# A decoder step on one Trainium2 core: the feed-forward gate and up products made as 2x2 block products with seven multiplications

## The reference, cut to what matters

```
x <- x + 1/2 * SwiGLU_1(RMSNorm(x))
x <- x + mixer(RMSNorm(x)) @ w_out          (attention branches and a pooling mixer)
x <- x + 1/2 * SwiGLU_2(RMSNorm(x))
y = RMSNorm_final(x)

def swiglu_ffn(x, g, w_gate, w_up, w_down):
    h = rmsnorm(x, g)
    return (jax.nn.silu(h @ w_gate) * (h @ w_up)) @ w_down
```

## Time and profile before

| | |
|---|---|
| median of 3 runs | 2870.1 us (2867.83 to 2872.59) |
| span of the profiled execution | 2868.9 us (no time of its own beside the span is given; it lies 1.2 us under the median) |
| stage `f1` | 456.7 to 1241.5 us |
| stage `f2` | 2078.0 us to the end |
| PE busy / DVE busy / ACT busy | 92% / 52% / 31% of the span |
| mean granted PE clock | 0.975 of full |

### The profile page before, as it was taken

One profiled execution on the slowest core, in us unless ns is written; L12 is line 12 of the kernel. 1 busy time (PEld: TensorE's weight loads), 2 busy tenths in 40 slices (PEclk: granted clock), 3 DMA queues, 4 the chain that ended last, 5 costly groups with the idle time before them and its releaser, 6 DMA issues. The chain is left out here.

```text
span 2868.9 us, 44901 instructions
## 1 busy us (share of the span) xinstructions
PE 2649.2 (92%) x17616; PEld 2498.9 (87%) x17616; DVE 1484.9 (52%) x2887; ACT 885.1 (31%) x1570; POOL 384.7 (13%) x427
## 2 busy tenths in 40 slices
PE   4999998999999999999978888777999999999997
PEld 4888887999999999988966666556999999999997
DVE  5444445554444444464147768555464444444445
ACT  4656655111111111032246656444221111111112
POOL 4444441000000000000012222452000000000001
PEclk9999999999999999999979979899999999999999
DMA  4131313211111110021311010586031111111101
GB/s 180 64 125 64 125 56 119 74 46 58 55 47 44 44 44 29 15 100 43 101 62 45 24 44 34 185 279 226 16 88 45 45 55 46 44 44 44 51 15 61
DMA packets 171831, 206.88 MB, mean 72 GB/s; under 512 B 15342, under 2 KB 153455, under 8 KB 169002
## 3 DMA queue, kind: packets, MB, share of 16 engines
q1 hardware_dynamic: 161026, 144.91, 16.3%
q0 software_dynamic: 10672, 60.19, 5.7%
HBM read 191.39 MB, written 18.01 MB: 73 GB/s over the span
## 5 line engine op out<-in xcount | busy, mean ns | idle before, releaser
L464 ACT ACTIVATE f_act_gate<-f_act_gate 128x352 f32<-128x352 f32 x132 | 65.8, 498 | 1185.3 <-DVE f_act_gate L572 1185.2
L589 DVE SCALAR_TENSOR_TENSOR trunk<-f_down,trunk 128x352 f32<-128x352 f32 x528 | 275.9, 524 | 205.3 <-PE f_down L114 205.3
L112 PE MATMUL f_down<-f_a_hi,f_wd_hi 128*128 128x352 f32 x1056 | 341.1, 323 | 0.0
L114 PE MATMUL f_down<-f_a_hi,f_wd_lo 128*128 128x352 f32 x1056 | 340.3, 322 | 0.0
L113 PE MATMUL f_down<-f_a_lo,f_wd_hi 128*128 128x352 f32 x1056 | 339.3, 321 | 0.0
L112 PE MATMUL cs_sum<-cs_x_hi,cs_w_hi 128*128 128x256 f32 (+1 forms) x768 | 230.3, 300 | 33.0 <-DVE cs_x_lo L1184 21.6
L114 PE MATMUL cs_sum<-cs_x_hi,cs_w_lo 128*128 128x256 f32 (+1 forms) x768 | 218.0, 284 | 0.0
L113 PE MATMUL cs_sum<-cs_x_lo,cs_w_hi 128*128 128x256 f32 (+1 forms) x768 | 217.6, 283 | 0.0
L1041 POOL TENSOR_TENSOR cs_x_lo<-cs_x,cs_x_hi 128x516 fp32r<-128x516 f32 x128 | 170.9, 1335 | 235.4 <-ACT cs_x_hi L1098 235.4
L114 PEld LDWEIGHTS f_down<-f_a_hi,f_wd_lo 128*128 128x128 f32 x1056 | 199.1, 189 | 0.0
L113 PEld LDWEIGHTS f_down<-f_a_lo,f_wd_hi 128*128 128x128 f32 x1056 | 198.7, 188 | 0.1
(11 more groups left out here) (421 smaller groups left out, 6745.6 us busy)
## 6 DMA issues: line engine op xcount, KB each, us to landing
f_gu_raw<-in_w_ffn_gate_dram SPq DMA_DIRECT2D x44, 512.0 KB, 4.3
f_gu_raw<-in_w_ffn_up_dram SPq DMA_DIRECT2D x44, 512.0 KB, 5.7
as_pages<-in_cache_kv_slc_dram SPq DMA_DIRECT2D x128, 128.0 KB, 4.0
as_pages<-in_cache_kv_slc_dram POOLq DMA_DIRECT2D x128, 128.0 KB, 4.0
at_spread<-saved_rows SPq DMA_DIRECT2D x16, 768.0 KB, 3.9
in_w_raw<-in_w_ffn_down_dram SPq DMA_DIRECT2D x11, 1024.0 KB, 5.0
f_wd_raw<-in_w_ffn_down_dram SPq DMA_DIRECT2D x11, 1024.0 KB, 5.0
x_saved<-trunk SPq DMA_DIRECT2D x2, 2112.0 KB, 14.8
```

Source lines behind the costliest of these rows:

```text
L112: pe.matmul(out, w_hi, x_hi, start=first, stop=False)
L114: return pe.matmul(out, w_lo, x_hi, start=False, stop=last)
L464: act.activation(act_gate[:, b, :], act_gate[:, b, :], ACT.Silu).then_inc(silu_done, 1)
L589: dve.scalar_tensor_tensor(xT[:, m, chunk(c)], down_bank[n % 4][:, 0:CH], 0.5, xT[:, m, chunk(c)], ALU.mult, ALU.add).then_inc(down_free, 1)
```

## The change

For one hidden tile the gate and up weights are four blocks: gate and up (two block rows), model channels 0 to 511 and 512 to 1023 (two block columns, `KH` = 4 k-tiles each). Token thirds 0 and 1 form the other 2x2 block matrix. Their product is made with seven block products on sums of blocks instead of eight; third 2 stays plain. So:

- Weights: eight forms of 4 k-tiles per hidden tile (four raw blocks and four sums or differences made on DVE by `sum_w`), each with its own high part (`high_w`, ACT) and low part (`low_w`, DVE), in a ring of four slots. Before it was 16 k-tiles with one high and one low instruction.
- Tokens: six block operands `b_sum` and a seventh, `last_sum`, made once per stage and kept on chip with their high and low parts (`high_b`, `low_b`), and `s_hi`, `s_lo` for third 2. They replace the `h_hi`, `h_lo` of all thirds, so the out-projection stage no longer makes those of thirds 0 and 1.
- PE: 7 x 12 matmuls for the blocks and 48 for third 2, 132 per tile; 264 + 144 per pair.
- Results: copies of two banks on ACT (`base`, `fifth`), five more additions on DVE per tile. The activation's high part goes from DVE to ACT (`high_a`).
- Order: the loops are written out for all 11 pairs. Between the steps of the activation DVE and ACT make the next tile's first four forms. Down products begin with third 1 (`order_of`), in the last pair with third 0, and each third waits for its `low_a` (`a_ready`).
- `f1_wd_lo` now lies in the memory of `in_w_raw`, so the input projection's first load waits for the last down product.
- The Newton step has one instruction less; the final norm's rows have a tile each.

The core of the diff, engine by engine. SP, the loads of a tile's weights and the next stage's first load:

```diff
+def load_half(v, j, k, split):
+    if v:
+        sp.wait_ge(w_lo_done, 8 * v - 8 + split)
+    sp.dma_start(gu_raw[:, j, k:k + KH], (wg_v, wu_v)[j][:, k:k + KH, v, :]).then_inc(
+        raw_landed[j][k // KH], 16)
+
+def load_raw(v):
+    load_half(v, 0, 0, 4)
+    load_half(v, 0, KH, 6)
+    load_half(v, 1, 0, 7)
+    load_half(v, 1, KH, 8)
...
+    sp.wait_ge(down_done, DOWNS * PAIRS)
+    sp.wait_ge(up_far_done, FT)
     sp.dma_start(next_load[0], next_load[1]).then_inc(next_landed, 16)
```

ACT, for each tile:

```diff
+def high_w(v, i):
+    n = 8 * v + i
+    if i in SUM_OF:
+        act.wait_ge(w_summed, 4 * v + SUM_OF[i][1])
+    else:
+        act.wait_ge(raw_landed[RAW_OF[i][0]][RAW_OF[i][1] // KH], 16 * v + 16)
+    if n >= 4:
+        act.wait_ge(product_done, event((n - 4) // 8, END[(n - 4) % 8]))
+    act.activation(w_hi[:, i % 4], form(i), ACT.Copy).then_inc(w_hi_done, 1)
...
+for g in range(FT):
+    act.wait_ge(product_done, event(g, 1))
+    if g:
+        act.wait_ge(act_done[0], g)
+    act.activation(base, bank_1, ACT.Copy).then_inc(first_copied, 1)
+    high_w(g, 4)
+    act.wait_ge(product_done, event(g, 3))
+    if g:
+        act.wait_ge(act_done[1], g)
+    act.activation(fifth, bank_5, ACT.Copy).then_inc(fifth_copied, 1)
+    high_w(g, 5)
+    high_w(g, 6)
+    if g == 0:
+        norm.root(act, 2)
+    high_w(g, 7)
+    if g % 2 == 0:
+        act.wait_ge(wd_landed, 16 * (g // 2) + 16)
+        act.activation(wd_hi[:], wd_raw, ACT.Copy).then_inc(wd_hi_done, 1)
+    silu(g, 0)
+    silu(g, 2)
+    silu(g, 1)
+    if g + 1 < FT:
+        high_w(g + 1, 0)
+    high_a(g, 1)
+    if g + 1 < FT:
+        high_w(g + 1, 1)
+        high_w(g + 1, 2)
+    high_a(g, 0)
+    if g + 1 < FT:
+        high_w(g + 1, 3)
+    high_a(g, 2)
```

DVE, ahead of the first tile:

```diff
+low_w(0, 0)
+with_first_half(1, 0, 1)
+low_b(0, 1)
+low_s(0)
+sum_w(0, 1)
+low_w(0, 1)
+dve.wait_ge(scaled, 2)
+dve.wait_ge(b_made, 1)
+dve.tensor_tensor(b_sum[:, 3], b_sum[:, 5], b_sum[:, 1], ALU.subtract).then_inc(b_made, 1)
+low_b(1, 2)
+with_first_half(2, 5, 2)
+sum_w(0, 2)
+low_w(0, 2)
+dve.wait_ge(b_made, 3)
+low_b(2, 3)
+if not prepared:
     norm.mean_square(dve, sum_bank, 0)
+sum_w(0, 3)
+low_w(0, 3)
+dve.wait_ge(scaled, 3)
+dve.wait_ge(b_made, 2)
+dve.tensor_tensor(last_sum[:], b_sum[:, 4], b_sum[:, 3], ALU.subtract).then_inc(b_made, 1)
+low_b(3, 4)
+if not prepared:
     norm.invert(dve, 0)
     norm.mean_square(dve, sum_bank, 1)
+dve.wait_ge(b_made, 4)
+low_b(4, 5)
+low_b(5, 6)
+low_b(6, 7)
+low_s(KH)
+if not prepared:
+    norm.invert(dve, 1)
```

DVE, for each tile:

```diff
+for g in (2 * q, 2 * q + 1):
+    more = g + 1 < FT
+    sum_w(g, 5)
+    low_w(g, 4)
+    low_w(g, 5)
+    low_w(g, 6)
+    if g == 0:
+        norm.mean_square(dve, sum_bank, 2)
+    dve.wait_ge(product_done, event(g, 5))
+    dve.wait_ge(first_copied, g + 1)
+    dve.tensor_tensor(base, base, bank_6, ALU.add).then_inc(base_done, 1)
+    dve.wait_ge(base_done, g + 1)
+    dve.tensor_tensor(above, base, bank_7, ALU.add).then_inc(above_done, 1)
+    low_w(g, 7)
+    if g == 0:
+        dve.wait_ge(above_done, 1)
+        norm.tmp = far
         norm.invert(dve, 2)
...
+    dve.wait_ge(above_done, g + 1)
+    dve.wait_ge(fifth_copied, g + 1)
+    dve.tensor_tensor(fifth, above, fifth, ALU.add).then_inc(up_far_done, 1)
+    dve.wait_ge(product_done, event(g, 6))
+    if g:
+        dve.wait_ge(a_ready[0], g)
+    dve.tensor_tensor(near, bank_1, inv[:, chunk(0)], ALU.mult).then_inc(gate_scaled[0], 1)
+    dve.wait_ge(product_done, event(g, 7))
+    if g:
+        dve.wait_ge(a_ready[2], g)
+    dve.tensor_tensor(third, bank_gate, inv[:, chunk(2)], ALU.mult).then_inc(gate_scaled[2], 1)
+    if g % 2 == 0:
+        dve.wait_ge(wd_hi_done, q + 1)
+        dve.tensor_tensor(wd_lo, wd_raw, wd_hi[:].bitcast(F32), ALU.subtract).then_inc(wd_split, 1)
+    rescale(g, 0)
+    rescale(g, 2)
+    dve.wait_ge(product_done, event(g, 8))
+    if g:
+        dve.wait_ge(a_ready[1], g)
+    dve.tensor_tensor(far, base, bank_5, ALU.add).then_inc(far_summed, 1)
+    dve.wait_ge(far_summed, g + 1)
+    dve.tensor_tensor(far, far, inv[:, chunk(1)], ALU.mult).then_inc(gate_scaled[1], 1)
+    if more:
+        sum_w(g + 1, 1)
+        low_w(g + 1, 0)
+    rescale(g, 1)
+    activate(g, 1, fifth, up_far_done, g + 1)
+    if more:
+        low_w(g + 1, 1)
+        sum_w(g + 1, 2)
+    dve.wait_ge(product_done, event(g, 10))
+    dve.wait_ge(far_summed, g + 1)
+    dve.tensor_tensor(base, base, bank_7, ALU.add).then_inc(up_near_done, 1)
+    activate(g, 0, base, up_near_done, g + 1)
+    low_a(g, 1)
+    if more:
+        low_w(g + 1, 2)
+        sum_w(g + 1, 3)
+    activate(g, 2, bank_up, product_done, event(g, 11))
+    low_a(g, 0)
+    if more:
+        low_w(g + 1, 3)
+    low_a(g, 2)
```

PE, for each tile (`strassen` and `plain` are 12 matmuls each, `begin` waits for the form's low part):

```diff
+def tile(g):
+    q, first = g // 2, g % 2 == 0
+    begin(g, 0)
+    if g and first:
+        pe.wait_ge(down_free, DOWNS * q - 1)
+    elif g:
+        pe.wait_ge(gate_scaled[0], g)
+    strassen(g, 0, 0, bank_1, True)
+    if g:
+        pe.wait_ge(gate_scaled[2], g)
+    plain(g, 0, 0, bank_gate, True)
+    if g == 0 and not prepared:
+        norm.total(pe, sum_bank, 1)
+    begin(g, 1)
+    if g:
+        pe.wait_ge(far_summed, g)
+    strassen(g, 1, 1, bank_5, True)
+    begin(g, 2)
+    if g:
+        pe.wait_ge(up_near_done, g)
+    strassen(g, 2, 2, bank_7, True)
+    begin(g, 3)
+    if g and first:
+        pe.wait_ge(down_free, DOWNS * q)
+    elif g:
+        pe.wait_ge(base_done, g)
+    strassen(g, 3, 3, bank_6, True)
+    if g == 0:
+        norm.total(pe, sum_bank, 2)
+    begin(g, 4)
+    pe.wait_ge(first_copied, g + 1)
+    strassen(g, 4, 4, bank_1, False)
+    plain(g, 4, KH, bank_gate, False)
+    begin(g, 5)
+    pe.wait_ge(fifth_copied, g + 1)
+    strassen(g, 5, 5, bank_5, False)
+    begin(g, 6)
+    if g:
+        pe.wait_ge(act_done[2], g)
+    plain(g, 6, 0, bank_up, True)
+    begin(g, 7)
+    pe.wait_ge(above_done, g + 1)
+    strassen(g, 7, 6, bank_7, False)
+    plain(g, 7, KH, bank_up, False)
```

More of the change, by code:

```diff
@@ L346, in stage_ffn @@
[L346 to L363, removed]
+            h_hi, h_lo, next_norm, next_gain, next_w, wd_lo, next_load, next_landed = ahead
@@ new lines, in stage_ffn @@
+        base, fifth, far, near = [mem.sb(scope, f"{name}_{part}", [P, CH])[:] for part in ("base", "fifth", "far", "near")]
+        above = spare_temp if ahead else mem.sb(scope, name + "_above", [P, CH])[:]
+        third = norm.var[:]
+        norm.tmp = above
+        doubles = [mem.ps(scope, f"{name}_bank{i}", (P, 2 * BANK)) for i in range(4)]
+        singles = [x[:, i * BANK:(i + 1) * BANK] for x in doubles for i in range(2)]
+        bank_1, bank_6, bank_5, bank_7, bank_gate, bank_up = [x[:, 0:CH] for x in singles[2:8]]
@@ new lines, in stage_ffn @@
+        down_done, down_free = mem.sem(name + "_down_done"), mem.sem(name + "_down_free")
+        gate_of = (near, far, third)
+        if ahead:
+            next_norm.sq = next_sq[:]
+        if finish:
+            flat_rows = b_sum[:].rearrange("p f k n -> p (f k n)")
+            rows = [flat_rows[:, t * D_MODEL:(t + 1) * D_MODEL] for t in range(TT - 1)]
+            rows.append(gu_raw[:, 0].rearrange("p k n -> p (k n)"))
+            fin.use([doubles[2 + t % 2] for t in range(7)] + doubles[0:2], rows)
@@ new lines, in scale, with high_b @@
+                def scale(i, c, k0):
+                    act.wait_ge(norm.gain_in, 16)
+                    for k in range(KH):
+                        last = act.activation(b_sum[:, i, k], xT[:, k0 + k, chunk(c)], ACT.Copy,
+                                              scale=norm.gain[:, k0 + k:k0 + k + 1])
+                    last.then_inc(scaled, 1)
+                def high_b(i, ready, count):
+                    act.wait_ge(ready, count)
+                    whole, high, _ = operand(i)
+                    act.activation(high, whole, ACT.Copy).then_inc(b_hi_done, 1)
@@ L514, in _ @@
                 if finish:
[L515 to L517 removed]
+                    act.wait_ge(product_done, event(FT, 0))
                     for t in range(6):
@@ new lines, in low_w, with with_first_half @@
+                def low_w(v, i):
+                    dve.wait_ge(w_hi_done, 8 * v + i + 1)
+                    dve.tensor_tensor(w_lo[:, i % 4], form(i), w_hi[:, i % 4].bitcast(F32),
+                                      ALU.subtract).then_inc(w_lo_done, 1)
+                def with_first_half(out, other, ready):
+                    dve.wait_ge(scaled, ready)
+                    for k in range(KH):
+                        made = dve.scalar_tensor_tensor(b_sum[:, out, k], xT[:, k, chunk(1)], norm.gain[:, k:k + 1],
+                                                        b_sum[:, other, k], ALU.mult, ALU.subtract)
+                    made.then_inc(b_made, 1)
@@ new lines, in low_b, with low_s @@
+                def low_b(i, count):
+                    whole, high, low = operand(i)
+                    dve.wait_ge(b_hi_done, count)
+                    dve.wait_ge(b_made, READ_BY[i])
```

(8 more changed lines are left out.)

585 lines of the change are left out of this document (281 added, 304 removed).

## The result

| | before | after |
|---|---|---|
| median | 2868.97 us (2867.60 to 2872.59, 4 runs) | 2895.18 us (2891.98 to 2897.52, 4 runs) |
| span of the profiled execution | 2868.9 us | 2892.3 us |

The ratio is 1.0088 with a 95% interval of 1.0073 to 1.0102: the kernel with fewer matmuls is 0.9% slower, 26 us.

What follows compares the result with a forecast made beforehand. Both feed-forward stages were taken as bound by PE. The span was 2868.9 - 28.0 + 37.3 + 6 + 10 = 2894 us, the median 2895 us (+0.9%), range 2852 to 2922.

Steps and rivals of the forecast that it cites:

- Step 1: Down phases: PE waits 2.43 us for low_a in each of ten pairs per stage; with fewer matmuls, net -28.0 us.
- Step 2: Stage heads: DVE's queue of operand preparation delays the first down products, +15.6 us in f1 and +21.7 in f2.
- Step 3: End of f1: the input projection's first load waits for the last down product, +6 us, between 4 and 8.
- Step 4: Down-phase gaps: PE's clock falls behind 6 of the 20, 1.7 us each, +10 us, between 0 and 34.
- (a): Rival at low_a of third 1: chain short enough, so faster; 2834 us with no gap at all; chance 0.24.
- (b): Rival at the down-phase gaps: the clock falls in most of them, 2916 us; chance 0.12.
- (c): Rival inside tiles: lows late at form 0 or 3, 1 us per tile more, 2938 us; chance 0.08.
- (d): Rival on PE: the 12 matmuls per tile not gone while the heads are paid, above 2950 us; chance 0.01.

Runs made afterwards that it cites:

- experiment 2: The kernel after, with fourteen idle matmuls filling PE's gap before the first down product in each stage's first ten pairs: 2884.74 us, ratio 1.0047 to the kernel before.
- experiment 1: The kernel after, with the second tile's activation made first and the next tile's forms spread between down-phase updates: 2837.65 us, ratio 0.9885 to the kernel before.
- experiment 3: The kernel after, with only form 1's low part and form 2's sum moved behind low_a of third 1: 2870.62 us, ratio 1.0000 to the kernel before.
- experiment 4: The kernel after, with a second equal subtraction on DVE before every low_b, 7 per stage: 2914.91 us, ratio 1.0151 to the kernel before.
- experiment 5: The kernel before, with the input projection's first load waiting for the last down product of f1: 2874.71 us, ratio 1.0015 to the kernel before.
- experiment 7: The kernel early_activation (next tile's forms made between updates), with low_b of token blocks 5 and 6 on GpSimd: 2836.98 us, ratio 0.9887 to the kernel before.

## Why the prediction was right

The median was forecast at 2895 and came at 2895.2. That it agrees this closely is luck: the span was forecast at 2894 and came at 2892.3, and the median then lay 2.9 us above the profiled span instead of 1.2. Term by term, in us of the profiled executions:

| step | forecast | measured | how |
|---|---|---|---|
| 1. ten periods and the last gap, clock aside | -28.0 | -28.0 | (682.29 - 690.73) + (680.97 - 691.33) - 6 x 1.53 |
| 2. heads | +37.3 | +37.8 | 15.95 + 21.82 |
| 3. first load | +6 | +4.5 | 4.47 from the last update of `f1` to `f2` (841.78 - 837.31), one execution each; 4.57 at the place |
| 4. clock | +10 | +9.2 | 6 x 1.53; some 10 by experiment 2 |
| rest (start of `f1`, tails) | 0 | -0.1 | |
| sum | +25 | +23.4 | 2892.3 - 2868.9 |

- **Step 1, the chain.** The links stood where they were put: from `far` to the down product 7.83 us, forecast 23.35 - 15.48 = 7.87. Experiments 1 and 3 show that it is the chain and not DVE's load. But the sum hides two errors that cancel. In `f1` the period before is 69.07, not 68.48: I had divided the span of eleven splits by ten, and the first of them is six microseconds late behind pair 0's extra work. The second and third, in the timeline of DVE before:

```profile
572.20 2.29 DVE L609 TENSOR_TENSOR f_wd_lo<-in_w_raw,f_wd_hi 128x2048 fp32r<-128x2048 f32 x1
641.27 2.28 DVE L609 TENSOR_TENSOR f_wd_lo<-in_w_raw,f_wd_hi 128x2048 fp32r<-128x2048 f32 x1
```

  They are 69.07 apart, the first (509.1) and the second only 63.1. The period after took over the same too small step per matmul (0.1585) and came at 67.86 instead of 67.20. Difference forecast 1.28, measured 1.21. In `f2` the first split is only 0.8 us late, and 69.05 stands for 69.13; difference forecast 1.32, measured 69.13 - 67.72 = 1.41. A period is to be read from neighbours, not from the first and the last event. The last gaps, 1.16 us idle, cost 66.95 - 65.52 = 1.43 us in `f1` and 66.78 - 65.17 = 1.61 in `f2`, with 1.41 forecast. The 0.1 us that PE was to wait at each pair's start does not show: in the undisturbed period of `f1` no step but the gap and the one behind it is over 0.17 us.
- **Step 2, the heads.** The count of DVE's instructions gave 83.4 and 72.5 us, the trace 83.75 and 72.65. The steps in between hold too: PE begins form 4 at 45.4 and 34.3 us (forecast 45.0 and 34.0) and tile 1 at 60.2 and 49.1 (60.0 and 49.0). The 34.0 is up to 0.7 more than its own terms give (2.6 + 26.1 + at most 4.6 = 33.3). Experiment 4 shows that each us added to DVE there is a us in the head.
- **Step 3, the load.** The mechanism is right (experiment 5 reproduces 5.41 us). The clock did fall behind it, as the window shows:

```profile
1255.40:1260.40 5.00, 4.95 (x17) 4.98 (x18) 5.00 (x13) 5.00 (x14) 0.00 (x0) 0.50 0.30 68
```

  Whether the 1.7 us forecast for that reach the end is not shown. One execution of each kernel gives 4.5 for the whole term, but the stretch behind it varies by several us from one execution to the next (experiment 5), so 4.5 and 6 can't be told apart.
- **Step 4, the clock.** Six of twenty was a guess from two of four, and that it came at just six is luck; that such gaps cost falls, and how much each, is shown by experiment 2. The rule of the Trainium skill that was weighed in the forecast (page "TensorE: Matmul & The Clock Gate", section "Why this matters for your kernels"; all of these gaps are shorter than what it asks to avoid) would have given 2885. The trace disagrees: the 5 us behind six of them were granted 0.66.
- **Rivals.** (a) was false for this order, yet its price was nearly right: with no gap 2834 was worked out, and experiment 1, which keeps a short gap in the last pairs, measured 2837.7. (b) and (c) did not come: fourteen gaps kept the clock, and in the ten periods of each stage no step over 0.34 us stands inside the tiles. (d) is out by the count: 528 products fewer, 408 matmuls per period.

## What to carry to other kernels

When a change makes the bounding engine wait for a product of others, write down the queue of each engine in the order of the code up to the releasing instruction: here six instructions on the next tile's weights (four on DVE, two on ACT) and two on another third stood ahead of the one that the down phase waited for, and cost 49 us of gaps (10 x 2.34 + 10 x 2.55) and 9 of clock. Put what the wait needs first and spread the rest between instructions that have slack; two pieces moved right behind it made the next wait and gave back only 0.6 to 0.8 us per pair. And one-time preparation on the second engine was paid in full in each stage's head, where PE had no other product to run.

## What the runs showed of the hardware that was not expected

- Which gap costs the clock is regular and not a matter of length alone: in `f1` of the kernel after the falls are behind the first, fifth and ninth gap, 272.98 us (four periods) apart each time, with gaps that are alike (steps of 2.39, the first 2.43); in `f2` behind the third, sixth and eighth. In experiment 4 it is again six, in `f1` behind the sixth and the tenth gap, 273.00 us apart. So of 40 gaps in two kernels (steps of 2.38 to 2.75 us, 2.1 to 2.4 idle) 12 made it fall, and the longest of each kernel, steps of 2.73 and 2.75, did not; of the 20 gaps of experiment 3 (steps of 1.72 us, 1.40 idle) none did. All this is from one profiled execution of each kernel. What picks them stays open.
- The step of a matmul is not the same in both stages: in experiment 1, without a gap, 65.52 / 408 = 0.1606 us in `f1` and 65.17 / 408 = 0.1597 in `f2`; before the change 69.07 / 432 = 0.1599 and 69.13 / 432 = 0.1600. This costs `f1` 0.3 us per pair. Its cause was not tried.
- GpSimd takes 3.2 us for 1408 columns in a subtraction. DVE's two-input instructions beside it grow by nearly as much (6.0 us beside 7.1 in `f2` of experiment 7); in `f1`, where a reciprocal of DVE, with one input, ran beside GpSimd's first, that one kept its 2.35 us.
